# Gate weights of every second expert as two transfers: 127 partitions and one

## The reference, cut to what matters

```python
def add_expert(acc, params):
    wg, wu, wd, c = params
    act = jax.nn.silu(h @ wg) * (h @ wu)
    return acc + (act @ wd) * c[:, None], None

out, _ = lax.scan(add_expert, jnp.zeros_like(h), (w_gate, w_up, w_down, combine))
```

## Time and profile before

| | us |
|---|---|
| median of three runs | 1111.4 |
| lowest and highest run | 1111.25, 1112.27 |
| the profiled execution | 1111.95 |
| its span, to which all rows of the trace refer | 1110.1 |
| TensorE busy in the span | 1044.4 |
| first load of expert weights asked for, at | 542.3 |
| last load of up weights in use, from | 1092.3 |

### The profile page before, as it was taken

One profiled execution on the slowest core, in us unless ns is written; L12 is line 12 of the kernel. 1 busy time (PEld: TensorE's weight loads), 2 busy tenths in 40 slices (PEclk: granted clock), 3 DMA queues, 4 the chain that ended last, 5 costly groups with the idle time before them and its releaser, 6 DMA issues.

```text
span 1110.1 us, 17677 instructions
## 1 busy us (share of the span) xinstructions
PE 1044.4 (94%) x6757; PEld 606.0 (55%) x6757; DVE 438.4 (39%) x1210; ACT 235.5 (21%) x545; POOL 302.4 (27%) x262
## 2 busy tenths in 40 slices
PE   6999999998999999899999599999999999998886
PEld 3644444445777777433565455555555555555553
DVE  3555888887565565523344311111111111111222
ACT  2113221121444446411021101111111111111011
POOL 1023412550554444103000112222222222221222
PEclk9999999999999999999999699999999999999999
DMA  6330232207476444897895789999999999999993
GB/s 209 98 112 21 77 106 96 104 2 272 145 241 218 121 138 137 330 387 249 337 413 202 284 327 417 414 418 414 415 414 417 416 414 415 415 417 416 418 407 117
DMA packets 85496, 304.39 MB, mean 274 GB/s; under 512 B 23452, under 2 KB 27676, under 8 KB 73506
## 3 DMA queue, kind: packets, MB, share of 16 engines
q1 hardware_dynamic: 67682, 273.47, 63.3%
q0 software_dynamic: 9824, 16.98, 5.3%
q10 hardware_dynamic: 7904, 12.78, 3.1%
HBM read 290.09 MB, written 29.72 MB: 288 GB/s over the span
## 4 chain that ended last, share of the span: by engine, by line
PE 40%; DMA 9%; SPq 7%; DVE 1%; issue 1%; ACT 0%; POOL 0%; POOLq 0%; ACTq 0%; DVEq 0%
PE e_Y L1893 7%; PE e_U L1879 7%; PE e_G L1879 7%; SPq L1101 6%; PE g_ring L1298 5%; DMA x_merged<-in_w_up 4%; PE e_TX L1873 4%; DMA x_up<-in_w_up 4%; PE g_S L1321 3%; PE g_P L1321 2%; DMA token_rows<-k_x 1%; PE x_O L1340 1%; SPq L1109 1%; PE x_O L1885 1%; DVE k_rows L2107 1%
## 5 line engine op out<-in xcount | busy, mean ns | idle before, releaser
L404 PE MATMUL p_z<-k_w,k_xT 128*128 128x512 f32 (+2 forms) x528 | 208.3, 549 | 0.1
L404 PEld LDWEIGHTS p_z<-k_w,k_xT 128*128 128x128 f32 (+1 forms) x528 | 92.0, 188 | 102.7 <-issue 101.1
L872 PE MATMUL a_G<-k_xT,k_w 128*128 128x260 f32 x512 | 127.5, 393 | 0.0
L2011 ACT ACTIVATE k_rows<-e_Y,x_share 64x512 f32<-64x512 f32 x64 | 43.7, 682 | 330.2 <-PE e_Y L1893 319.6
L872 PEld LDWEIGHTS a_G<-k_xT,k_w 128*128 128x128 f32 x512 | 93.1, 192 | 26.5 <-issue 13.6
L2098 DVE SCALAR_TENSOR_TENSOR k_rows<-e_G,x_share,k_rows 128x256 f32<-128x256 f32 x32 | 15.5, 484 | 232.7 <-ACT k_rows L2006 232.7
L967 POOL TENSOR_TENSOR k_x<-k_x 128x512 f32<-128x512 f32 x64 | 80.5, 1271 | 89.6 <-DVE k_side L1033 69.3
L2138 POOL DMA_INDIRECT out_y_p<-k_rows,x_table x32 | 46.2, 1444 | 178.9 <-ACT k_rows L2011 173.7
L157 POOL DMA_INDIRECT k_rows<-token_rows,x_halves x32 | 33.8, 1056 | 174.1 <-PE e_TX L1873 159.9
L1873 PEld LDWEIGHTS e_TX<-k_c,k_rows 64*64 64x64 f32 x1024 | 64.0, 212 | 14.9 <-issue 12.6
L1873 PE MATMUL e_TX<-k_c,k_rows 64*64 64x64 f32 x1024 | 68.4, 285 | 2.2 <-DMA k_rows<-token_rows,x_halves 2.2
(11 more groups left out here) (369 smaller groups left out, 1532.6 us busy)
## 6 DMA issues: line engine op xcount, KB each, us to landing
k_w<-in_w_in SPq DMA_DIRECT2D x11, 2048.0 KB, 8.4
k_w<-in_w_gate SPq DMA_DIRECT2D x8, 2048.0 KB
k_w<-in_w_up SPq DMA_DIRECT2D x8, 2048.0 KB
k_xT<-in_w_down SPq DMA_DIRECT2D x8, 2048.0 KB
k_oT<-in_w_gate SPq DMA_DIRECT2D x8, 2048.0 KB, 31.6
k_side<-in_w_up SPq DMA_DIRECT2D x8, 2048.0 KB
x_page<-in_w_down SPq DMA_DIRECT2D x8, 2048.0 KB
x_w_out<-in_w_gate SPq DMA_DIRECT2D x8, 2048.0 KB
```

The costliest lines, as they stand in the source:

```text
L404: last = nc.tensor.matmul(z[u % 3][0:p, 0:WIDTH[k]], s.xT[:, j, 128 * i:128 * i + p], s.w[:, c % 2, j, 0:WIDTH[k]], start=j == 0, stop=j = ...
L872: last = nc.tensor.matmul(G[u % 2][:, 0:HT], s.w[:, q % 2, j, 128 * c:128 * c + 128], s.xT[:, j, HT * h:HT * h + HT], start=j == 0, stop=j ...
L2011: last = nc.scalar.activation(y[j][:, W * h:W * h + W], Y[j][CAP * h:CAP * h + CAP, :], ACT.Copy, scale=s.share[CAP * h:CAP * h + CAP, 0, ...
```

## The change

A load by `load_expert` of gate weights into place 1 or 3 (`LAST_ALONE`) is now asked for as two transfers, one right behind the other: partitions 0 to 126, and then partition 127. Both add 16 to the same semaphore, and the count that TensorE waits for is doubled for those places. The other loads are as before, and so are all products, places and waits of the loads.

```
+PARTITIONS = ([slice(0, 128)], [slice(0, 127), slice(127, 128)])
+LAST_ALONE = lambda n, r: n == 0 and r % 2 == 1
...
 def load_expert(eng, io, s, e, n):
 
     r = e % DEPTH[n]
     for b, part in s.ew[n][r]:
-        eng.dma_start(part, s.expert(io[EXPERT_WEIGHTS[n]], e, n)[:, b:b + part.shape[1], :]).then_inc(s.ew_in[n][r], 16)
+        rows = s.expert(io[EXPERT_WEIGHTS[n]], e, n)[:, b:b + part.shape[1], :]
+        for p in PARTITIONS[LAST_ALONE(n, r)]:
+            eng.dma_start(part[p], rows[p]).then_inc(s.ew_in[n][r], 16)
...
 def weights_in(s, e, n):
 
-    r, parts = e % DEPTH[n], len(s.ew[n][e % DEPTH[n]]) + 2 * ((n, e % DEPTH[n]) == (2, FIRST))
+    r, parts = e % DEPTH[n], len(s.ew[n][e % DEPTH[n]]) * len(PARTITIONS[LAST_ALONE(n, e % DEPTH[n])]) + 2 * ((n, e % DEPTH[n]) == (2, FIRST))
     return s.ew_in[n][r], 16 * (FIRST_LOADS.get((n, r), parts) + parts * (e // DEPTH[n]))
```

## The result

The changed kernel takes 2377.5 us (median; 2373.4 to 2380.3) where the kernel before took 1111.8 us in the same comparison: 2.137 times as long, with an interval of 2.133 to 2.141. The forecast was 2183 us with a range of 2130 to 2270, so the direction was right and the time lies 194 us above the forecast and outside the range.

A forecast was written before the change was run, and what follows sets the result against it. The experts' stage was taken to be bound by the 16 DMA engines' transfers. Span 1110.1 + 1091 (127 rows) + 4 (last row) - 28 (idle filled) + 4 (tail) = 2181, plus 1.85 around it: 2183 us, range 2130 to 2270.

The forecast's parts named there:

- One engine takes all 127 rows, always the same one: Split gate loads: 127 rows can't be shared equally over 16 engines, so one carries all; the same each time was assumed.
- Price of a row: A 16 KB row takes one engine 0.611 us; 119 rows more per split make 72.7 us, 1091 us in 15 loads.
- The last row: Partition 127's own transfer: 0.6 to 9 us for 15 loads, taken as 4.
- The engine never runs dry: SyncE has about 100 us for a gate request and needs some 10, so nothing is added and prefetch hides nothing.
- term 3: Loads behind a 127-row transfer wait for it; the stage becomes the sum of one engine's work, the other 15 counting nothing.
- the sign that engine time stays the same: Experts' stage after the change: the same 528 us of busy time per engine in some 1620 us, mean share near 0.33.
- The upper bound from the stage's mean rate: Pricing the 127 rows at 26.0 GB/s for an engine: 75.0 us a load, 1125 us in all.
- What it fills: DMA idle time in the experts' stage, while loads waited for `merge`, goes: 22 to 34 us saved, taken as 28.
- The tail: From the last up weights' landing to the end, products slow after TensorE's idle time: 0 to 5.4 us more, taken as 4.
- A: Rival: 127-row transfers fall on different engines in turn and overlap; about 1230 to 1445 us, chance 0.06.
- B: Rival: 127 rows dealt unevenly, 8 to fifteen engines and 7 to one; 1111.5 to 1121 us, chance 0.07.
- C: Rival: a stalled SyncE issue holds up ScalarE's stores in `merge`, the engine idles; 20 to 60 us over forecast, chance 0.07.

The follow-up runs named there:

- the bench: Bench in place of the kernel: five loads of 128 rows, then 127 rows in one queue took 104.24 us; 127 rows first, then the five, 117.27 us.
- the added wait: Changed kernel, but SyncE waits until each load of 127 and 1 partitions has landed before asking for the next load: 2230.2 us.

## Why the prediction was right, and where it was wrong

*One engine takes all 127 rows, always the same one.* Right. The completions of the earlier trace rows had been read correctly; 79.5 us for 127 rows against 7.8 for 128, and a rate of 26 GB/s at 6.1% of 16 engines show it directly. That it is always the same one follows from the pairs, which don't overlap.

*Price of a row, 0.611 us from the earlier trace rows.* Right as long as the engine works alone: 0.61 us in the quiet stretch, and 104.24 us for the plain sum in the bench.

*The last row.* One completion, so one engine, the upper end of my bounds: up to 9 us in all where I took 4.

*The engine never runs dry.* Right as far as the sum tells: 104.9 us of a pair as forecast, 0.6 for the last row and 13 for the five loads beside it make 118.5, and nothing is left for idle time. The prefetch of four experts gave nothing back; the single split of expert 17 cost more than its work.

*"What the other 15 engines do in that time is worth nothing."* **This is the step that failed** (term 3). It is worth less than nothing. The 15 others do the five loads behind the long transfer while it runs, and the long transfer's rows cost more meanwhile: 0.87 us and not 0.61 over the 46 us counted above. That is 2.6 us for each load of 128 rows by the bench's two orders, 13 of the 13.6 us of a pair, and the added wait takes most of it away. It also broke the sign that engine time stays the same: it grew by 1110 us in queue q1. My sum priced each engine's rows as if engines could not disturb each other, and the rows I rested it on, and the earlier trace rows, came from stretches of whole loads of 128 rows, where a row costs 0.61 us with all 16 engines at work. The upper bound from the stage's mean rate (1125 us and not 1091) did not cover it for the same reason. That the slowing is a meeting of engines at one place in SBUF is shown by the benches for short loads (same rows read, other partitions); for the long transfer it is argued from them.

*What it fills, 28 us.* About right: without expert 1's split the kernel is 53 us faster, where 72.7 + 13 - 28 makes 58.

*The tail.* Forecast 4 us more; from the start of the last gate product to the end it is 22.9 us and was 22.6 in the kernel before, so next to nothing. The 6.24 us of the earlier trace rows I had misread besides: TensorE had been idle only 0.80 us before that product, not for tens of us. The slower gate product (5.60 us) only took the place of the wait for the up weights that stood there. Of the 194 us, 176 are the pairs, and the tail took 4 less than forecast. The remaining 22 fall before expert 5's gate product (812.59 us); the two split loads up to there would make 26 at 13 us each, but I have not taken that stretch apart.

*Rivals.* A and B are out by the benches. C's delay was there (45 us later into the experts' stage), but the split that causes it cost 53 us, not more than the 58 that work, slowing and filling make without it.

## What to carry to other kernels

Ask of every transfer by SyncE or ScalarE how its row count divides (127 puts all on one engine, and everything queued behind waits for it) and which partitions the engines write at the same time: a full DMA busy share with half the GB/s is the mark of engines in each other's way, and even 64 and 64 or 120 and 8 rows cost 10 to 14 us for each load here. When a sum adds up work per engine, take its prices once from a stretch with neighbours of the new kind, or give the range that room.

## What I had not expected of the hardware

- An added wait made the kernel faster: with the long transfer running alone 2230 us, with 15 engines working beside it 2378 us.
- 16 rows for 16 engines cost 2.3 us in neighbouring partitions and 1.2 us spread, against 0.61 us undisturbed.
- 127 rows asked for by GpSimd take 12.5 us, where SyncE's and ScalarE's take 79.5 and 79.9 us.
- SyncE stood 62.83 us in one issue, and later requests that have nothing to do with the long transfer stood behind it.
